# Parts of the first normalised X taken straight from PSUM, and the sparse attention's first scores issued between query tiles

## The reference

```python
def rmsnorm(x, g):
    y = x32 * lax.rsqrt(jnp.mean(x32 * x32, axis=-1, keepdims=True) + EPS)
    return (y * g).astype(x.dtype)
```

```python
p_cmp = masked_softmax(einsum(q, k_cmp) * scale, cmp_end <= pos)
o = gates[0] * (p_cmp @ v_cmp) + gates[1] * o_sel + gates[2] * o_win
```

## Time and profile before

| | |
|---|---|
| median of 3 runs | 2924.21 us (2922.79 to 2929.07) |
| the profiled execution | 2932.94 us |
| its span in the trace | 2931.2 us |
| TensorE busy / VectorE / ScalarE / GpSimd | 97% / 47% / 27% / 69% of the span |
| mean granted TensorE clock | 0.986 of 2.4 GHz |

### The profile page before, as it was taken

How to read it: one execution, slowest core, us unless ns; L and a number is a source line. 1 busy time by engine, 2 the same in 40 slices (tenths; PEclk the granted TensorE clock), 3 DMA queues, 4 the chain that set the end, 5 groups by cost and what they waited for, 6 DMA issues and landing times.

```text
span 2931.2 us, 38634 instructions
## 1 busy us (share of the span) xinstructions
PE 2848.2 (97%) x13970; PEld 2304.2 (79%) x13970; DVE 1383.1 (47%) x2003; ACT 791.6 (27%) x1451; POOL 2035.6 (69%) x2346
## 2 busy tenths in 40 slices
PE   7999999999989999999899999999999999999998
PEld 5887888878756788887777778888877777888887
DVE  4746666126476566622664554222065554632302
ACT  2232222014466322211424332111032344211100
POOL 5747899779735688877754467777785545877774
PEclk8999999999989999999999999999999999999999
DMA  3212323223200123332221122323322122222332
GB/s 133 66 50 83 97 93 100 93 93 115 79 8 2 58 94 100 93 101 93 80 65 58 59 85 93 100 94 98 96 90 76 58 65 65 95 100 93 100 94 93
DMA packets 66361, 242.55 MB, mean 83 GB/s; under 512 B 7488, under 2 KB 7616, under 8 KB 66240
## 3 DMA queue, kind: packets, MB, share of 16 engines
q1 hardware_dynamic: 66240, 240.95, 25.5%
HBM read 238.82 MB, written 2.10 MB: 82 GB/s over the span
## 4 chain that ended last, share of the span: by engine, by line
PE 89%; DVE 7%; POOL 2%; issue 1%; ACT 1%; DMA 0%; DVEq 0%; SPq 0%; ACTq 0%
PE bank L475 25%; PE bank L477 25%; PE bank L476 25%; PE bank L885 1%; POOL w_lo L451 1%; PE bank L856 1%; DVE XL L1563 1%; PE bank L1012 1%; PE bank L845 1%; PE bank L1050 1%; PE bank L590 1%; PE bank L977 1%; DVE ss L1575 1%; PE bank L1024 1%; PE bank L958 1%
## 5 line engine op out<-in xcount | busy, mean ns | idle before, releaser
L451 POOL TENSOR_TENSOR w_lo<-w_raw,w_hi 128x256 fp32r<-128x256 f32 x1784 | 1485.4, 863 | 35.7
L448 POOL CAST w_hi<-w_raw 128x1024 fp32r<-128x1024 f32 x446 | 484.1, 1086 | 745.2 <-DMA w_raw<-weights_dram 744.7
L475 PE MATMUL bank<-XH,w_hi 128*128 128x512 f32 x2416 | 963.9, 399 | 25.9 <-DVE XL L1563 12.2
L477 PE MATMUL bank<-XH,w_lo 128*128 128x512 f32 x2416 | 947.3, 392 | 0.0
L476 PE MATMUL bank<-XL,w_hi 128*128 128x512 f32 x2416 | 947.1, 392 | 0.0
L475 PEld LDWEIGHTS bank<-XH,w_hi 128*128 128x128 f32 x2416 | 457.3, 189 | 131.8 <-DVE XL L1563 22.3
L477 PEld LDWEIGHTS bank<-XH,w_lo 128*128 128x128 f32 x2416 | 457.2, 189 | 97.4
L476 PEld LDWEIGHTS bank<-XL,w_hi 128*128 128x128 f32 x2416 | 457.9, 190 | 94.5 <-issue 2.7
L1586 DVE TENSOR_TENSOR X<-X,bank 128x512 f32<-128x512 f32 x64 | 43.8, 684 | 513.4 <-PE bank L477 513.0
L477 PE MATMUL bank<-hid_h,w_lo 128*128 (+1 forms) x704 | 273.9, 389 | 0.0
L475 PE MATMUL bank<-hid_h,w_hi 128*128 (+1 forms) x704 | 273.9, 389 | 0.0
(11 more groups left out here) (338 smaller groups left out, 3424.9 us busy)
## 6 DMA issues: line engine op xcount, KB each, us to landing
w_raw<-weights_dram SPq DMA_DIRECT2D x446, 512.0 KB, 3.4
x_tok<-x_dram SPq DMA_DIRECT2D x4, 512.0 KB, 5.1
out_dram<-y_tok SPq DMA_DIRECT2D x4, 512.0 KB, 2.8
const_sb<-consts_dram SPq DMA_DIRECT2D x1, 834.0 KB, 11.4
par_sb<-params_dram SPq DMA_DIRECT2D x1, 665.0 KB, 9.9
masks_in<-masks_dram SPq DMA_DIRECT2D x1, 640.0 KB, 12.5
y_gain<-gain_out_dram SPq DMA_DIRECT2D x1, 512.0 KB, 4.6
const_sb<-consts_dram SPq DMA_DIRECT2D x1, 129.0 KB, 2.2
```

The costliest lines, as they stand in the source:

```text
L448: nc.gpsimd.tensor_copy(w_hi[s][:, :, :], w_raw[s][:, :, :]).then_inc(s_hi, 1)
L451: ins = nc.gpsimd.tensor_tensor(w_lo[s][:, rows, :], w_raw[s][:, rows, :], w_hi[s][:, rows, :].bitcast(F32), ALU.subtract)
L475: nc.tensor.matmul(out_ap, w_hi[slot][:, j, :], xh, start=start, stop=False)
L477: return nc.tensor.matmul(out_ap, w_lo[slot][:, j, :], xh, start=False, stop=stop)
```

## The change

Three things. (1) ACT makes XH from bank k, DVE makes XL from bank k, X is copied afterwards (except the first), together with the sums of squares; the squares come after all of XH on ACT. Tiles 0 to 3 wait until the bank they write has been copied to X. `stats(0)` moves from behind tile 0 to behind tile 2, the gate matmuls from behind tile 2 to behind tile 3. (2) Jobs 0 to 3 of the sparse attention are issued between query tiles: scores 0 and 1 after tile 7, 2 and 3 after tile 8, with two small buffers of their own for the weights of jobs 0 and 1. `query(6)` and `query(7)` come after scores 6. (3) The compressed softmaxes of rounds 2 and 3 move in among the jobs: on DVE before jobs 8, 12 and 16, on ACT at 10, and their transposes on PE before jobs 20 and 28, into the banks of the jobs' transposes. Round 3 takes bank 0 for its scores. The first turn moves from tile 5 to 6, the second from 7 to 8. The bodies of `copied`, `scores`, `score_max` and `score_weights` are those of before, made functions and called earlier; in the cut below they are left out, as are the removed lines of PE's job loop.

```diff
@@ -189,6 +189,12 @@
         masks_bf = at("masks_bf", [P, MASKS, P], BF16, o_masks)
         causal_bf, sb_neg_bf = masks_bf[:, 8, :], masks_bf[:, 9, :]
         ident_bf = small("ident_bf", [P, P], BF16)
+        def weights_of(m):
+            return n_P_first[m] if m < 2 else n_P[m % 6]
+        CS_BANK = (6, 7, 6, 0)
+        CMP_TURN_JOB = (16, 24)
         def query_tile(job):
@@ -281,6 +287,7 @@
         n_PT = at("n_PT", [P, 2, 4, TT, P], F32, o_A + 14592)
         n_P = [at(f"n_P{s}", [P, T], F32, o_A + 18688 + s * T) for s in range(6)]
+        n_P_first = [at(f"n_P_first{s}", [P, P], F32, o_N + 2304 + s * P) for s in range(2)]
         n_sc = [at(f"n_sc{s}", [P, T], F32, o_A + 2048 + s * T) for s in range(2)]
         n_pcT = at("n_pcT", [P, 4, T], F32, o_A)
         n_cst = small("n_cst", [P, 3, 16])
@@ -661,10 +668,12 @@
                 for t in range(17):
                     if t >= 4:
                         pe.wait_ge(gs["evac"], t - 3)
+                    else:
+                        pe.wait_ge(s_x, t + 1)
                     tile(u0 + t, t % 4, XH, XL, s_xl if t == 0 else None)
-                    if t == 0:
+                    if t == 2:
                         stats(0)
-                    if t == 2:
+                    if t == 3:
                         pe.wait_ge(gs["evac"], 1)
                         pe.wait_ge(s_rstd, 1)
@@ -777,11 +786,13 @@
                     pe.wait_ge(ns["evac"], U_NSA_KV + 1 + e + 1)
                     if e == 0:
                         pe.wait_ge(ns["kvcc"], 5)
-                    if e % 2 == 0 and rd >= 2:
-                        pe.wait_ge(ns["csub"], rd - 1)
+                    if e == 4:
+                        pe.wait_ge(ns["csub"], 1)
+                    if e == 6:
+                        pe.wait_ge(ns["rope"], 12)
                     for c in range(TT):
                         lo_ = c * P + e % 2 * 64
-                        mm = nc.tensor.matmul(bank[6 + rd % 2][:, lo_:lo_ + 64], raw[:, c * P:(c + 1) * P], n_kc[:, rd, :, :],
+                        mm = nc.tensor.matmul(bank[CS_BANK[rd]][:, lo_:lo_ + 64], raw[:, c * P:(c + 1) * P], n_kc[:, rd, :, :],
                                               start=True, stop=True)
                     mm.then_inc(ns["cs"], 1)
@@ -794,6 +805,50 @@
...
+                    elif q == 2:
+                        pe.wait_ge(ns["csub"], 3)
...
+                def transposed(m):
+                    pe.wait_ge(ns["w"], m + 1)
+                    if m == 1:
+                        pe.wait_ge(ns["pTc"], 2)
+                    if m == 2:
+                        pe.wait_ge(ns["rope"], 4 + 7)
+                    if m >= 3:
+                        copied(m - 3)
+                    if m in CMP_TURN_JOB:
+                        pe.wait_ge(ns["pTc"], CMP_TURN_JOB.index(m) + 3)
+                    for j in range(query_tile(m) + 1):
+                        mm = nc.tensor.transpose(bank[1 + m % 3][:, j * P:(j + 1) * P], weights_of(m)[:, j * P:(j + 1) * P], ident)
+                    mm.then_inc(ns["t"], 1)
                 u0 = START["nsa_q"]
                 for t in range(U_NSA_Q):
@@ -806,67 +861,33 @@
...
                         compressed()
                         pe.wait_ge(ns["evac"], U_NSA_KV + 1)
                         turn(5, n_raw[:, 0, :], ns["gT"])
+                    if 2 <= t < 8:
                         query(t - 2)
+                    if t == 6:
                         pe.wait_ge(ns["gate"], 1)
+                        cmp_turn(0, 5)
+                    if t == 7:
+                        pe.wait_ge(s_bf, 2)
+                        pe.wait_ge(ns["kld"], 4)
+                        pe.wait_ge(ns["pTc"], 1)
+                        scores(0)
+                    if t == 8:
+                        pe.wait_ge(ns["rope"], 4 + 6)
+                        cmp_turn(1, 2)
+                        scores(2)
+                for q in range(4, jobs + 8, 2):
+                    if q - 4 in CMP_TURN_JOB:
+                        copied(q - 7)
+                        cmp_turn(2 + CMP_TURN_JOB.index(q - 4), 1 + (q - 4) % 3)
                     if q < jobs:
                         scores(q)
+                    if q < jobs + 4:
                         transposed(q - 4)
                         transposed(q - 3)
+                    if q == 6:
+                        query(6)
+                        query(7)
                     if q >= 10 and q % 4 == 2:
                         n = (q - 10) // 4
                         e, i = n // 4, query_tile(4 * n)
@@ -874,9 +895,11 @@
                         copied(4 * n + 2)
                         copied(4 * n + 3)
                         if n % 4 == 0:
-                            pe.wait_ge(ns["pTc"], 4)
+                            pe.wait_ge(ns["pTc"], g + 1)
                             if e:
                                 pe.wait_ge(ns["o"], e)
+                            else:
+                                pe.wait_ge(ns["csub"], 4)
                             nc.tensor.matmul(bank[0][:, :], n_bd[:, g, e % 2, :], n_pcT[:, g, :], start=True, stop=False,
                                              skip_group_check=True)
                         for j in range(i + 1):
@@ -1188,7 +1211,11 @@
                                          bank[4][:, :].rearrange("p (c k) -> p c k", c=TT), ACT.Copy).then_inc(gs["vc"], 1)
                 nc.scalar.preload_act_table_set("natural_log_exp_and_others")
-                prepare(0)
+                for k in range(KT):
+                    act.wait_ge(s_xt, k + 1)
+                    nc.scalar.activation(XH[:, k, :], bank[k][:, :], ACT.Copy, scale=parts_gain(0, k)).then_inc(s_xh, 1)
+                for k in range(KT):
+                    squares(0, k)
                 inv_rms(0)
                 for c in range(TT):
@@ -1352,23 +1379,34 @@
                     act.wait_ge(ns["rope"], 4 + e + 1)
                     nc.scalar.activation(n_qh[:, e, :], n_rot[e % 2][:, :], ACT.Copy).then_inc(ns["qh"], 1)
+                jobs = NSA_HEADS * TT * 2
+                def score_exp(q):
+                    S = (query_tile(q) + 1) * P
+                    if q >= 6:
+                        act.wait_ge(ns["t"], q - 5)
+                    act.wait_ge(ns["mx"], q + 1)
+                    nc.scalar.activation(weights_of(q)[:, 0:S], bank[4 + q % 4][:, 0:S], ACT.Exp, bias=n_st[:, 0, q:q + 1],
+                                         accum_out=n_st[:, 1, q:q + 1]).then_inc(ns["exp"], 1)
                 for e in range(8):
                     if e:
                         q_high(e - 1)
                     swap(e)
                     if e in (3, 5, 7):
                         cmp_exp((e - 3) // 2)
-                    if e in (4, 6):
-                        cmp_copy((e - 4) // 2, 5)
-                cmp_exp(3)
-                jobs = NSA_HEADS * TT * 2
-                for q in range(jobs + 9):
-                    if q == 5:
-                        cmp_copy(2, 0)
-                    if q == 9:
-                        cmp_copy(3, 0)
-                    if q == 2:
+                    if e == 5:
+                        cmp_copy(0, 5)
+                    if e == 6:
+                        score_exp(0)
+                        score_exp(1)
+                    if e == 7:
+                        cmp_copy(1, 2)
+                for q in range(2, jobs + 9):
+                    if q == 4:
                         q_high(7)
+                    if q == 10:
+                        cmp_exp(3)
                     if 5 <= q < jobs + 5 and (q - 5 < POOL_WEIGHS or q % 2):
                         m = q - 5
                         n, i = m // 4, query_tile(m)
@@ -1378,13 +1416,10 @@
                         nc.scalar.activation(n_PT[:, n % 2, m % 4, 0:i + 1, :],
                                              bank[1 + m % 3][:, 0:(i + 1) * P].rearrange("p (j t) -> p j t", t=P), ACT.Copy)\
                             .then_inc(ns["tc"], 1)
+                    if q - 4 in CMP_TURN_JOB:
+                        cmp_copy(2 + CMP_TURN_JOB.index(q - 4), 1 + (q - 4) % 3)
                     if q < jobs:
-                        S = (query_tile(q) + 1) * P
-                        if q >= 6:
-                            act.wait_ge(ns["t"], q - 5)
-                        act.wait_ge(ns["mx"], q + 1)
-                        nc.scalar.activation(n_P[q % 6][:, 0:S], bank[4 + q % 4][:, 0:S], ACT.Exp, bias=n_st[:, 0, q:q + 1],
-                                             accum_out=n_st[:, 1, q:q + 1]).then_inc(ns["exp"], 1)
+                        score_exp(q)
                     if q >= 24 and (q - 24) % 16 == 0:
                         e = (q - 24) // 16
                         act.wait_ge(ns["pv"], 4 * e + 4)
@@ -1959,20 +2013,29 @@
                         dve.wait_ge(ns["gate"], 1)
                         if e % 2 == 0:
                             cmp_scores(e // 2 - 1)
-                        elif e:
```

(112 more changed lines are left out.)

23 lines of the change are left out of this document (1 added, 22 removed).

## The result

The changed kernel takes 2909.62 us in the median (2904.73 to 2911.57, 6 runs), the one before 2924.24 us beside it. The medians differ by 14.6 us. The ratio is 0.9945 with a 95% interval of 0.9935 to 0.9955: 16.1 us less, between 13 and 19. Forecast were 17.2 us less and a time of 2907.0.

A forecast was written before the change was run, and what follows sets the result against it. TensorE, busy in 97% of the span, bounds the kernel, so only its waits and low clock could pay. Gains of 12.7 us (start) and 4.5 us (sparse attention) sum to 17.2, giving 2907.0 us; range 2902.6 to 2916.2.

The forecast's parts named there:

- The start: First projection, up to tile 4: XH and XL from PSUM and later statistics let tile 4 start 12.7 us sooner.
- nine matmuls at the low clock: Tile 0 of the first projection: about 9 matmuls cost 0.43 us and not 0.23, so it ends at 22.4 us.
- A tile 0 that is wholly at the low clock: First projection's lower case: tile 0 ends at 24.8 us and the start gains 10.5 us.
- The XL step: Start, on DVE: one XL from PSUM takes 0.69 us, with an upper bound of 1.15.
- The rival in which the squares hold tile 3: Start: copies and sums stay near 3.0 us a step, statistics wait 7 us, total gain 10 us; chance 0.08.
- the 13.6 us sum: Start: XL from PSUM doesn't contend with POOL, unit 0 is split 0.7 us sooner, and the gain is 13.6 us.
- The sparse attention: Sparse attention's start, up to scores 20: waits removed less new waits and moved softmaxes gain 4.5 us.
- the walk: Sparse attention followed step by step from query tiles to scores 20, which start at 842.2 us against 847.30 before.
- The wait of scores 0: Sparse attention: scores 0 wait 2.3 us for the first compressed copy, which ACT makes after swap 5 and an exp.
- The marks: Signs in both parts that would confirm the forecast, such as statistics starting at 33 to 35 us, or refute it.
- A second part that gives nothing: Sparse attention: new waits and DVE's load take all of the 4.5 us, total gain 10.7 to 12.7; chance 0.14.
- Slower by a clock that stays low: Tiles 0 to 3, perhaps sparse attention too: PE stays at 1.2 GHz, total 10 us slower, 2934; chance 0.03.

The follow-up runs named there:

- that part alone: Only the start's changes (XH and XL from PSUM, statistics and gate matmuls moved) against the kernel before: 2914.94 against 2927.94 us, ratio 0.9959.
- the repeat: The changed kernel profiled and timed once more, nothing altered: ratio 0.9955 to the kernel before, tile 4 at 43.77 us.
- XL-from-SBUF: The changed kernel with each X copied before its XL and XL made from the SBUF copy; run once, tile 4 at 46.86 against 42.67 us.
- the part alone: Only the sparse attention's changes, with the start of before, against the kernel before: 2922.16 against 2927.94 us, ratio 0.9986.
- copies ahead: The changed kernel with ScalarE's first two copies of compressed weights put ahead of q_high and the half swap: ratio 0.9947 to the kernel before.

## Why the prediction was right or wrong

**The start** was right in mechanism and size: 12.7 us forecast, 13.3 in the profile, 12.0 (8 to 16) by the ratio of that part alone. Tile 0 was to begin at 15.1 and end at 22.4; it began at 14.84, and matmul 25 followed at 21.9 without a gap. I took nine matmuls at the low clock; there were seven in this profile and fourteen in the repeat. (A tile 0 that is wholly at the low clock would end at 25.4 by 24 steps of 0.43 us, and not at 24.8 as the forecast has it; that takes 0.6 us off its 10.5 and changes no bound of the range.) The XL step was taken as 0.69 and was 0.67. The sum of squares was to be complete at 31.7 and was at 27.75: the sums without XL between them took 0.6 to 0.9 us, not 1.18. The rival in which the squares hold tile 3 therefore failed by far, and POOL's first splits were not late. w_lo of unit 0 took 2.78 us where XL has one SBUF operand, 3.70 with two in the XL-from-SBUF run, and a later unit 4.66 beside the sums. The Trainium skill (SBUF — State Buffer, "Who interferes with whom") says that a DVE instruction with two SBUF inputs contends with one of POOL that reads SBUF, and that one with at most one SBUF input doesn't, outside the modes that use two ports; the prediction left that exception out. These runs agree on two inputs against one. They also have a case beyond the short form of the rule: in the XL-from-SBUF kernel the copy ss<-sq, with one SBUF input, took 1.26 us beside a w_hi that took 1.50, while in the changed kernel it took 0.66. Whether that is the exception is not shown, since the traces don't have an instruction's mode. The 0.7 us that the 13.6 us sum takes off the split of unit 0 came (2.78 against 3.47), but this profile's split began 0.4 us later, so tile 0 began only 0.27 us sooner. That 13.3 lies nearer to 13.6 than to 12.7 is luck: the nine profiles with the new start have tile 4 at 41.2 to 43.8 us, 42.5 in the mean, against 55.6 for the two with the old, which is 13.0 us.

**The sparse attention** is the term that was mis-sized: 4.5 us forecast, 2.2 us in the profile, 2.8 in the part alone, and 2.5 between the means. The runs by themselves (4.1 us, 1.5 to 6.7) would allow 4.5. The order of events was right, down to the waits at scores 0 and transposition 1. Where the walk (the forecast's times followed) went wrong shows against its own marks, in us after query 3:

| | walk | changed | changed, again |
|---|---|---|---|
| scores 0 start | 16.8 | 18.1 | 18.1 |
| tile 8 ends | 24.6 | 27.1 | 25.9 |
| scores 6 start | 32.8 | 35.1 | 33.8 |
| scores 20 start | 58.2 | 60.5 | 59.3 |

Two steps failed, both ahead of scores 6. The wait of scores 0 was put at 2.3 us and is 4.0, which makes scores 0 1.3 us late. I had counted 0.6 us for every DVE step, while some of those beside POOL's splits took 1.1 to 1.2; that these steps are the whole of it is not shown:

```profile
780.12 1.12 DVE L1892 TENSOR_TENSOR n_t<-n_t,n_t 128x512 f32<-128x512 f32 x1
781.15 1.22 DVE L1953 TENSOR_TENSOR n_ql<-n_rot,n_qh 128x512 fp32r<-128x512 f32 x1
785.77 0.69 DVE L1974 TENSOR_REDUCE n_cst<-n_sc 128x16 f32<-128x512 f32 x1 [3.39 <-ACT n_sc L1367]
```

The clock after it was to be low for 3.4 us; in this profile it was low for over 5 us in tile 8, some 1.2 us more of lateness, which the repeat doesn't have. Behind scores 6 the walk was right: 25.4 us to scores 20, measured 25.45, and 0.5 us for the fourth turn, measured 0.6. That is partly luck. The walk has scores 8 6.4 us behind scores 6 and scores 20 19.0 behind scores 8, measured were 7.5 and 17.9. I had also charged no low clock there, and it was low from 799.5 to 817. The kernel before had a like stretch (0.59 at 821 to 830, 0.70 to 835.6). How long it lasted made no difference: the mean granted clock from scores 6 to scores 20 was 0.74 in the changed kernel and 0.78 with the copies ahead, and both took 25.5 us. Between scores 6 and 8 it was 0.50 in all ten kernels with the changed attention, so what it costs there is not shown. DVE, busy for 22.9 of them, was the bound, as forecast. The three waits of DVE for the exponentials I never priced. They are in both kernels and so no term of the difference, but the experiments show that they, and not TensorE's waits, were what the stretch hung on.

**The marks** I had set: tile 0 ends at 22 to 25 us (21.9), statistics 33 to 35 (32.9, from the chain), each 0.1 us early; gate matmuls end 42 to 45 (42.67), scores 20 about 5 us earlier (2.8, and 3.1 between the means: a miss), DVE over 90% busy behind scores 0 (20.1 of 22 us at 802 to 824, the same stretch in this profile), waits of 2 to 3 us at scores 0 (4.0: outside) and a like one at transposition 1 (3.0). "w_lo of units 1 and 2 under 4 us" was right for unit 1 and wrong for unit 2 (4.66). "Any later stretch changes by over 1 us" was a bad mark: equal code moved by 2.3 us and 4.2 us here, and by 5.4 between profiles.

**The rivals.** A second part that gives nothing is excluded by its own ratio (0.9977 to 0.9995). Slower by a clock that stays low: in the start the clock came back within tile 0 in the changed kernel and its repeat. In the sparse attention it did happen in part, for some 17 us, and turned nothing round.

## What to carry to other kernels

When TensorE's waits in a stretch have several causes that change places as soon as one is removed, look for the repeated wait on the engines that alternate behind it: here VectorE's 3.4 us for a 0.6 us exponential that stood behind 2.6 us of copies in ScalarE's queue. Here ordering a queue by who waits for each result gave more (5.9 us in the profiles) than moving TensorE's work (2.5 us). And compare stretches, not spans: 723 to 728 us of equal code differed by more between profiles than this second gain is worth, while shorter stretches agreed to 0.1 us. In the start the gain came from making the first operand straight from where it lies, with copies and sums put behind it and their consumer two tiles later.
